# A three-layer Trainium2 kernel: the second mixer's head norm by tile, its gate by column halves, its sixth block by seven products, the attention powers by tile

## What is computed

```python
def odd_mixer(h, w_in, conv_w, conv_b, gate_b, ml_norm_g, w_out):
    p = h @ w_in                         # 1024 x (2*512 + 2*1024 + 8)
    qk, v, og, ig_pre, fg_pre = split(p)
    ...                                  # convolution, gates, 4 heads of q, k: 128, v: 256
    out = mlstm_scan(q, k, v, lf, ig)    # scores @ v, divided by max(|den|, exp(-m))
    y = sigmoid(og) * head_rmsnorm(out, ml_norm_g, 4)
    return y @ w_out                     # 1024 x 1024
x = x + rmsnorm(y, g[1])                 # then the MLP of the layer

q = partial_rope(rms_norm(to_heads(q), g_q), cos, sin)   # 8 heads of 64, second block
k = partial_rope(rms_norm(to_heads(k), g_k), cos, sin)
```

## Time and profile before

| | us |
|---|---|
| median of 3 runs | 1515.87 (1515.13 to 1516.6) |
| the profiled execution, time | 1517.84 |
| the profiled execution, span of the trace | 1516.0 |
| TensorE matmuls busy | 1288.1 (85%) |
| VectorE / ScalarE / GpSimd busy | 556.9 / 213.6 / 83.6 |
| odd mixer, start of OD 0 to `keep_warm` | 457.09 to 595.38 |
| first expert load issued | 994.76 |

### The profile page before, as it was taken

One profiled execution on the slowest core, in us unless ns is written; L12 is line 12 of the kernel. 1 busy time (PEld: TensorE's weight loads), 2 busy tenths in 40 slices (PEclk: granted clock), 3 DMA queues, 4 the chain that ended last, 5 costly groups with the idle time before them and its releaser, 6 DMA issues.

```text
span 1516.0 us, 13525 instructions
## 1 busy us (share of the span) xinstructions
PE 1288.1 (85%) x5752; PEld 794.3 (52%) x5752; DVE 556.9 (37%) x732; ACT 213.6 (14%) x357; POOL 83.6 (6%) x77
## 2 busy tenths in 40 slices
PE   7999999999999989999999989998846636646656
PEld 4856747885456754888444778655412212212212
DVE  5478422546344732246545475414101001001001
ACT  3321301110011411111001114111100000000000
POOL 0047100000010001000001100000000000000000
PEclk9999999999999999999999999998968878878788
DMA  8633335884443333486453433476699999999997
GB/s 320 182 123 111 112 125 208 281 323 167 172 167 111 111 117 133 173 301 248 176 188 135 147 131 111 143 331 256 276 429 428 428 427 428 428 428 428 427 428 287
DMA packets 93612, 376.81 MB, mean 249 GB/s; under 512 B 6992, under 2 KB 7664, under 8 KB 81648
## 3 DMA queue, kind: packets, MB, share of 16 engines
q1 hardware_dynamic: 92832, 373.80, 63.6%
q0 software_dynamic: 576, 2.10, 0.4%
q10 hardware_dynamic: 144, 0.04, 0.0%
HBM read 374.88 MB, written 1.05 MB: 248 GB/s over the span
## 4 chain that ended last, share of the span: by engine, by line
PE 71%; DMA 18%; DVE 5%; ACT 2%; issue 2%; SPq 1%; POOL 1%; POOLq 0%; DVEq 0%; ACTq 0%
PE PS L861 15%; PE PS L871 13%; PE PS L672 11%; PE PS L714 8%; PE PS L655 7%; DMA normalised<-in_w 6%; DMA weights<-in_w 6%; PE PS L1086 5%; DMA proj_rows<-in_w 3%; PE PS L1122 3%; DMA arena<-in_w 2%; PE PS L620 2%; PE PS L1050 1%; SPq L482 1%; PE PS L1058 1%
## 5 line engine op out<-in xcount | busy, mean ns | idle before, releaser
L861 PE MATMUL PS<-normalised,weights 128*128 128x256 f32 x1024 | 223.7, 382 | 2.1 <-DVE normalised L1510 2.1
L861 PEld LDWEIGHTS PS<-normalised,weights 128*128 128x128 f32 x1024 | 195.9, 192 | 29.7 <-DVE normalised L1510 2.7
L1086 PE MATMUL PS<-weights,x_rows 128*32 128x512 f32 x400 | 140.9, 713 | 68.8 <-DMA proj_rows<-in_w 36.6
L871 PE MATMUL PS<-weights,arena 128*128 128x512 f32 x384 | 167.4, 592 | 0.0
L1086 PE MATMUL PS<-arena,x_rows 128*32 128x512 f32 x304 | 114.6, 713 | 57.6 <-DMA weights<-in_w 56.3
L672 PE MATMUL PS<-weights,normalised 128*128 128x256 f32 x696 | 157.1, 383 | 4.0 <-DVE weights L1555 3.3
L672 PEld LDWEIGHTS PS<-weights,normalised 128*128 128x128 f32 x696 | 132.6, 192 | 26.5 <-issue 7.3
L714 PE MATMUL PS<-weights,arena 128*128 128x512 f32 x288 | 126.9, 600 | 4.9 <-issue 4.1
L655 PE MATMUL PS<-weights,normalised 128*128 128x512 f32 x288 | 127.7, 602 | 3.7 <-DVE normalised L1510 2.2
L871 PEld LDWEIGHTS PS<-weights,arena 128*128 128x128 f32 x384 | 73.0, 190 | 91.0 <-issue 90.9
L1086 PE MATMUL PS<-proj_rows,x_rows 128*32 128x512 f32 x224 | 88.8, 719 | 33.1 <-DMA normalised<-in_w 33.1
(11 more groups left out here) (316 smaller groups left out, 1436.6 us busy)
## 6 DMA issues: line engine op xcount, KB each, us to landing
weights<-in_w SPq DMA_DIRECT2D x36, 2048.0 KB, 30.0
weights<-in_mlp_w SPq DMA_DIRECT2D x32, 2048.0 KB, 7.9
arena<-in_w SPq DMA_DIRECT2D x29, 2048.0 KB, 29.7
proj_rows<-in_w SPq DMA_DIRECT2D x18, 2048.0 KB, 29.8
proj_rows<-in_w_ada SPq DMA_DIRECT2D x12, 2048.0 KB, 8.1
weights<-in_ev_w_in SPq DMA_DIRECT2D x10, 2048.0 KB, 8.6
weights<-in_w_in SPq DMA_DIRECT2D x10, 2048.0 KB, 7.9
normalised<-in_w SPq DMA_DIRECT2D x9, 2048.0 KB, 31.8
```

The source lines that it names most:

```text
L861: last = mm(PS[:, 4 + 2 * h + j // 2, (j % 2) * T:(j % 2 + 1) * T], wn(s)[:, k, j * P:(j + 1) * P], HT[:, k, :], start=(k == 0), stop=(k = ...
L871: last = mm(PS[:, bank, :], lhs[:, k0 + i, rows], rhs[:, i, :], start=(g == 0 and i == 0), stop=(g == NGRP - 1 and i == 1))
L1086: last = mm(PS[CAP * x:CAP * (x + 1), 4 + kind, :], XG[:, k, CAP * x:CAP * (x + 1)], w[:, k, :], start=(k == 0), stop=(k == KT - 1), tile_ ...
```

## The change

It has two parts.

In the odd mixer, OD 5 becomes a block of seven products; its weight sums stand on VectorE behind the score products. `values` reports tile 0 (`ml_tile0`) before it goes on to tile 1, and the denominators of the two tiles lie in two banks. Division, squares, powers and the two multiplies are done by tile; the squares are eight activations with an accumulator, four a tile, which replace one activation and the reduction. ScalarE's order is: squares of tile 0, first partial read of OD 5, squares of tile 1, the other three reads, `finish`. The gate is applied by column halves: half 0 needs OD 4 alone, half 1 needs OD 5. TensorE transposes half 0 of both tiles, does the first output block (its tile 1 waits for the banks of OD 5), transposes half 1, and does the second output block.

In the attention, the power of 32 columns becomes two of 16, and VectorE waits for the second only before tile 1.

```diff
-SEVEN = (... + [B_OD_IN + b for b in range(1, 4)] + B_IN2_AT[1:])
+SEVEN = (... + [B_OD_IN + b for b in (1, 2, 3, 5)] + B_IN2_AT[1:])
-MIX_OD = [(4, 0, 2048, 0), (5, 0, 2560, 4), (6, 1, 2048, 0), (7, 1, 2560, 4)]
+MIX_OD = [(4, 0, 2048, 0), (6, 1, 2048, 0), (5, 0, 2560, 4), (7, 1, 2560, 4)]
@@ gpsimd
-            power(16, 24, RV_D, "sums_ready", 3)
+            for tt in range(TT):
+                power(16 + 4 * tt, 20 + 4 * tt, RV_D, "ml_sq", tt + 1)
...
-            power(128, 160, AD, "sums_ready", 4)
+            for tt in range(TT):
+                power(128 + 16 * tt, 144 + 16 * tt, AD, "sums_ready", 3)
@@ tensor, out_block(..., tile1_banks=None)
                 for tt in range(TT):
+                    if tt and tile1_banks is not None:
+                        pe.wait_ge(sem("proj_taken"), tile1_banks)
@@ tensor, values(col, n, dens=None, tile0=None)
+                    if tt == 0 and tile0 is not None:
+                        last.then_inc(sem(tile0), 1)
@@ tensor
-            values(1024, 2, dens=PS[:, 0, 0:8])
-            proj_block(B_OD_IN + 5)
-            mixed_T(MIX_OD, "od_y_half", (1, 1, 2, 2))
-            pe.wait_ge(sem("proj_taken"), EV_IN + OD_IN)
+            values(1024, 2, dens=PS[:, 0:2, 0:4], tile0="ml_tile0")
+            seven_block(B_OD_IN + 5)
+            mixed_T(MIX_OD[:2], "od_y_half", (1, 2))
+            pe.wait_ge(sem("mix_T"), 8)
+            out_block(B_OD_OUT, YT, 0, True, False, tile1_banks=EV_IN + OD_IN)
+            mixed_T(MIX_OD[2:], "od_y_half", (3, 4))
             pe.wait_ge(sem("mix_T"), 10)
-            for i in range(OD_OUT):
-                out_block(B_OD_OUT + i, YT, 4 * i, i == 0, i == OD_OUT - 1)
+            out_block(B_OD_OUT + 1, YT, 4, False, True)
@@ scalar
-            act.wait_ge(sem("ml_o"), 1)
-            a(XN[:, :, :], HB.rearrange("p (a b) -> p a b", a=2), ACT.Square).then_inc(sem("mix_sq"), 1)
-            evac(5 * NB, ACT.Sigmoid)
+            def head_squares(tt):
+                act.wait_ge(sem("ml_o"), tt + 1)
+                for h in range(4):
+                    ...
+                    last = a(XN[:, tt, at], HB[...], ACT.Square,
+                             accum_out=ST[:, 16 + 4 * tt + h:17 + 4 * tt + h])
+                last.then_inc(sem("ml_sq"), 1)
+            head_squares(0)
+            part(B_OD_IN + 5, 0)
+            head_squares(1)
+            for i in range(1, 4):
+                part(B_OD_IN + 5, i)
+            finish(B_OD_IN + 5, 5 * NB, ACT.Sigmoid)
@@ vector
-            dve.wait_ge(sem("mix_out"), 3)
-            ...
+            col_sums(B_OD_IN + 5)
+            last_sum(B_OD_IN + 5)
+            for tt in range(TT):
+                ...wait for ml_tile0 or mix_out 3, denominators of 4 heads, division of 128x1024, ml_o tt + 1
+            for tt in range(TT):
+                rstd()
+                ...multiply by the roots, multiply by the gains, 128x1024 each
+            for half in range(2):
+                if half:
+                    part_sums(B_OD_IN + 5, 5 * NB)
+                dve.wait_ge(sem("proj_taken"), EV_IN + 5 + half)
+                for tt in range(TT):
+                    gate = PR[:, tt, 2048 + half * NB:2560 + half * NB]
+                    tell(v.tensor_tensor(gate, gate, tile[tt][:, half * NB:(half + 1) * NB], ALU.mult),
+                         "od_y_half", 2 * half + tt + 1)
```

More of the change, by code:

```diff
@@ L82 @@
                + B_IN2_AT)
-SEVEN = ([B_EV_IN + b for b in (1, 2, 3, 8, 9)] + [B_OD_IN + b for b in range(1, 4)]
+SEVEN = ([B_EV_IN + b for b in (1, 2, 3, 8, 9)] + [B_OD_IN + b for b in (1, 2, 3, 5)]
          + B_IN2_AT[1:])
@@ L705, in modulation, with out_block @@
                 last.then_inc(sem("mod_raw"), 1)
-            def out_block(b, lhs, k0, first, last_k, bank=0, mark=True):
+            def out_block(b, lhs, k0, first, last_k, bank=0, mark=True, tile1_banks=None):
                 s = slot_of(b)
@@ L819, in scores, with values @@
                         .then_inc(sem("score_raw"), 1)
-            def values(col, n, dens=None):
+            def values(col, n, dens=None, tile0=None):
                 pe.wait_ge(sem("score_p"), 4 * n)
@@ L832, in values @@
                             for i, (left, st) in enumerate(parts):
-                                last = mm(dens[:, 4 * tt + h:4 * tt + h + 1], left, ONE[:, 0:1],
+                                last = mm(dens[:, tt, h:h + 1], left, ONE[:, 0:1],
                                           start=(i == 0), stop=(i == len(parts) - 1))
+                    if tt == 0 and tile0 is not None:
+                        last.then_inc(sem(tile0), 1)
                 last.then_inc(sem("mix_out"), 1)
@@ L1352, in _ @@
             evac(4 * NB, ACT.Sigmoid)
-            act.wait_ge(sem("ml_o"), 1)
-            a(XN[:, :, :], HB.rearrange("p (a b) -> p a b", a=2), ACT.Square).then_inc(sem("mix_sq"), 1)
-            evac(5 * NB, ACT.Sigmoid)
+            def head_squares(tt):
+                act.wait_ge(sem("ml_o"), tt + 1)
+                for h in range(4):
+                    at = slice(h * RV_D, (h + 1) * RV_D)
+                    last = a(XN[:, tt, at], HB[:, tt * D + h * RV_D:tt * D + (h + 1) * RV_D], ACT.Square,
+                             accum_out=ST[:, 16 + 4 * tt + h:17 + 4 * tt + h])
[6 more added lines that the diff above has]
+            finish(B_OD_IN + 5, 5 * NB, ACT.Sigmoid)
             mix_evac(MIX_OD)
@@ L1846, in _ @@
                                             ALU.mult, ALU.mult), "score_p", 4 + h + 1)
-            dve.wait_ge(sem("mix_out"), 3)
[L1849 to L1859, removed]
+            col_sums(B_OD_IN + 5)
+            last_sum(B_OD_IN + 5)
+            tile = [HB[:, tt * D:(tt + 1) * D] for tt in range(TT)]
@@ new lines, in _ @@
+            for tt in range(TT):
+                if tt == 0:
+                    dve.wait_ge(sem("ml_tile0"), 1)
+                else:
+                    dve.wait_ge(sem("mix_out"), 3)
+                den, top = ST[:, 128 + 4 * tt:132 + 4 * tt], ST[:, 120 + 4 * tt:124 + 4 * tt]
+                link(v.scalar_tensor_tensor(den, PS[:, tt, 0:4], -1.0, top, ALU.mult, ALU.max))
+                link(v.tensor_tensor(den, PS[:, tt, 0:4], den, ALU.max))
+                link(v.reciprocal(den, den))
+                tell(v.tensor_tensor(tile[tt].rearrange("p (g d) -> p g d", g=4),
+                                     PS[:, 4 + 2 * tt:6 + 2 * tt, :].rearrange("p b (h d) -> p (b h) d", h=2),
+                                     colb(den, RV_D), ALU.mult), "ml_o", tt + 1)
@@ new lines, in _ @@
+            for tt in range(TT):
+                rstd()
+                heads = tile[tt].rearrange("p (g d) -> p g d", g=4)
+                link(v.tensor_tensor(heads, heads, colb(ST[:, 16 + 4 * tt:20 + 4 * tt], RV_D), ALU.mult))
+                link(v.tensor_tensor(heads, heads, midb(HN[:, 384:640], 4), ALU.mult))
+            for half in range(2):
[6 more added lines that the diff above has]
+                         "od_y_half", 2 * half + tt + 1)
@@ L1876, in _ @@
             part_sums(IN[1], NB)
-            dve.wait_ge(sem("mix_sq"), 4)
+            dve.wait_ge(sem("mix_sq"), 3)
             v.tensor_reduce(ST[:, 128:160], HB.rearrange("p (g d) -> p g d", d=AD), AX.X, ALU.add)\
```

## The result

| | before | after |
|---|---|---|
| median of 5 runs, us | 1515.13 (1514.96 to 1516.6) | 1508.58 (1504.25 to 1508.94) |
| ratio after / before | | 0.9944, 95% interval 0.9931 to 0.9957 |
| the profiled execution's span, us | 1516.0 | 1502.5 |

The changed kernel is faster, by 6.6 us in the medians and by 0.56% (8.5 us) in the ratio. Over all runs the same two programs spread more than that table shows: the kernel before from 1508.83 to 1517.84, the changed one from 1504.25 to 1509.97. The profiled execution belongs to the lowest times of the changed kernel, and the profiled one of before to the highest of its own. So the 13.5 us between the two spans is not the change alone, and it pays to take it apart by stage.

The account below looks back on a forecast made before the run. Expert weights pace the last third, TensorE's order of work everything before. Savings of 5.5 (odd mixer) + 2.7 (attention) = 8.2 take the profiled 1517.84 to 1509.6; the median, 1.97 lower, gives 1507.5 us, range 1502.5 to 1511.5.

Parts of the forecast that it names:

- Part 1 on TensorE: Odd mixer, OD 5 to `keep_warm`: block of seven, transpositions and two output blocks, 12.09 + 2.68 + 13.81 + 1.82 + 13.81 us.
- The covers of part 1: Odd mixer: gates 2.5 us ahead of transpositions, ScalarE's second read 0.5 to spare, gain row 2.9 in hand; cost 0.
- The gain row's upper bound: Odd mixer: the gain row's DMA lands in 3.9 to 6.2 us, at 582.5 at the latest, before VectorE asks at 585.4.
- Part 1's worth: Odd mixer: `keep_warm` starts at 589.89 instead of 595.38, 5.5 us less; bounds 2.5 and 6.
- The bound of 2.5: Odd mixer: gain left if the clock falls again in the first idle stretch, costing 1.3 + 1.7 = 3.0 us.
- Part 2: Attention: two powers of 16 columns start IN 4 2.5 us earlier; 2.7 with faster transpositions, bounds 1 and 6.
- The 0.2 that was added for transpositions no longer slow: Attention: 0.2 us gained because the transpositions ahead of IN 4 leave low clock, added to the 2.5.
- IN 4's clock: Attention: with an idle of 2.1 us left before it, IN 4 keeps its 2.1 us of low clock.
- The median: Whole kernel: median of the runs forecast at 1507.5 us, from 8.2 saved and runs 1.97 below the profiled execution.
- The rival that the clock is kept: Attention and the norm behind each mixer: clock holds, 2.1 and about 3 us more saved, 1502.5 to 1505.5; chance 0.30.
- The slower rival: GpSimd powers in both mixers: each costs per instruction, so two more powers slow the kernel to 1520.5 us; chance 0.04.
- the gain lost in the stream: Expert stage: held by something other than its release, so most of 8 us is lost, 1515 us; chance 0.06.

Follow-up runs that it names:

- e2: The kernel before with only the attention's power of 32 columns made as two of 16; median 1511.92 us, ratio 0.9978 to before.
- e7: The changed kernel with IN 3's three weight sums ahead of the attention's reduction on VectorE instead of behind it; 1505.60 us (one run).
- e1: The changed kernel with the attention's powers in one piece of 32 columns again, odd-mixer edits kept; median 1509.18 us, ratio 0.9968 to before.
- e8: e7 with the attention's reduction also made in two halves, by tile; 1505.66 us (one run).
- e4: The changed kernel, unchanged, traced and timed again; median 1508.70 us, ratio 0.9962 to before.
- e5: The changed kernel with OD 5 as a plain block again, without its weight sums and partial sums; 1509.84 us (one run).
- e3: The changed kernel with unread 128x256 matmuls in TensorE's idle stretches (odd mixer, both later norms, before IN 4); median 1502.89 us, ratio 0.9926 to before.
- e11: The same kernel as e3, run again on the same chip as e10; median 1503.83 us, ratio 0.9921 to before.
- e9: e3 with the attention's weight sums ahead of the reduction and the reduction by tile; median 1504.95 us, ratio 0.9920 to before.
- e10: The kernel before with unread 128x256 matmuls in the same kinds of idle stretch as e3; median 1507.38 us, ratio 0.9948 to before.
- e6: The kernel before with OD 5 by seven products alone, the norm still for all heads at once; 1512.26 us (one run).

## Why the prediction was right, and where it was not

The forecast was 1507.5 with 1502.5 to 1511.5; measured 1508.58. Point by point:

- **Part 1 on TensorE**: right to 0.05 (44.21 and 44.26), because the likeness at the end of the second block's mixer was the same sequence with the same waits.
- **The covers of part 1**: all held; slack of 2.1, 0.9 and 2.3 where 2.5, 0.5 and 2.9 were counted. The gain row's upper bound was 0.6 too low: the landing of 6.2 before stood beside a load issued 2.8 earlier, with the DMA engines 0.96 busy, this one of 6.8 beside a load issued 1.8 earlier, at 0.97.
- **Part 1's worth**: the 5.5 was subtracted from a stage that had one low-clock stretch in this one execution. I treated that as the stage's length. e2 shows 47.1 with the same instructions and the same idle stretch, so the term with the clock kept is 2.85, and the other 2.6 is not in every execution. The low clock was priced too high as well: 1.3 + 1.7 = 3.0 was said, and against e2 it is 0.8 from the transpositions to the output block (3.96 and 3.13) and 1.8 in the output blocks (29.3 and 27.55). The bound of 2.5, which I gave for a *new* fall of the clock, comes near 2.85 for another reason. The 0.34 between `keep_warm` and the MLP (with the clock kept) was in no term.
- **Part 2**: the wait, 2.5, was right to 0.01, and e7 shows its reason, GpSimd held out by VectorE's operations with two SBUF inputs. The Trainium skill's page "SBUF — State Buffer", section "Who interferes with whom", has that rule, and here the trace agrees: 0.21 alone, 1.11 to 1.25 beside such an operation. The 0.2 that was added for transpositions no longer slow is worth nothing: in e1 they take 3.68 and IN 4 still starts 19.74 after IN 3, because VectorE's chain sets its start.
- **IN 4's clock**: I argued from the idle length, 2.1 between 1.65 and 2.45. An idle 2.45 went both ways (fallen in the trace of before, kept in e2's), and so did the changed kernel's 2.15: IN 4 took 12.25 in one trace and 13.94 in the other. Of the six traces with that idle 2.15 the clock was kept in four (after, e2, e7, e8) and fell in two (e4, e5). The length of one idle stretch does not decide it.
- **The median**: the stage sum with the clock held is 5.7, the ratios give 8.5 and 5.8 in two sets of runs (0.9944 and 0.9962). The second agrees with the stage sum; what the first has beyond it may be low clock that the change takes away on average, but that was not counted over many traces and is not shown. That the forecast, 8.2 below the profiled execution, came within 1.1 of the median is therefore luck in part: 2.6 of the 8.2 is a low-clock stretch of one trace. From 1515.87 the 5.7 alone gives 1510.2, still inside the range.
- **The rival that the clock is kept** happened in the profiled execution (span 13.5 less) and not in most others: two of the eleven times of the changed kernel lie at or below 1505.5. The slower rival is out: two powers of 4 columns cost 1.0 each. So is the gain lost in the stream: from the first expert load to the end it is 521.24 before, 519.29 and 521.46 after.

## What to carry to other kernels

Before you subtract a stage's length in one trace from a forecast, look at the granted clock in that stretch and price it both ways. The kernels with their idle stretches filled by unread matmuls were faster here; that they are a steadier ruler is not shown (e3 and e11 spread over 3.0 in ten runs, the changed kernel over 5.7 in eleven, but e9, filled alike, over 6.5 in six). Splitting a chain by tile and column half paid twice here, once by itself and once by letting a shorter neighbour count; the shorter neighbour alone bought nothing. In this kernel a power on GpSimd was shortest where VectorE had no operation with two SBUF inputs.

## What was not expected of the hardware

- With unread small matmuls in idle time (13 in e3, 21 in e10), at no cost in any stage of the table, the median was 5.8 us lower for the changed kernel and 7.9 for the kernel before.
- The stage from `keep_warm` to the MLP is 0.34 longer in the odd mixer of before (10.55 in e2 and e10, where the clock was kept) than in the changed kernel (10.21). In the chain it is a pause of VectorE between the power and the multiply that it had waited for, first in the kernel before, then in the changed one:

```profile
597.61 0.03 issue
597.64 0.02 DVEq L1491
597.66 0.41 issue
598.07 1.29 DVE normalised L1527
```

```profile
593.57 0.03 issue
593.60 0.02 DVEq L1511
593.62 0.06 issue
593.67 1.29 DVE normalised L1547
```

The instruction is the same. e6, which has before's norm in a program of another length, has 10.19. What makes the pause was not tried and stays open.
